# Latent attention: vector work of later head pairs on Pool, and an earlier split of the second output weight

## The reference, cut to what matters

```python
def mla(h, cos, sin, w_down, q_norm, w_uq, kv_norm, w_ukv, w_o):
    d = h @ w_down                                        # 384 + 128 + 64 columns
    cq = rms_norm(d[..., :Q_LORA_RANK], q_norm)
    ckv = rms_norm(d[..., Q_LORA_RANK:Q_LORA_RANK + KV_LORA_RANK], kv_norm)
    k_rope = apply_rope(d[..., Q_LORA_RANK + KV_LORA_RANK:], cos, sin)
    q = (cq @ w_uq).reshape(B, S, N_HEADS, QK_HEAD_DIM)   # per head 128 plain, 64 rotary
    q_rope = apply_rope(q[..., QK_NOPE_DIM:], cos[:, :, None], sin[:, :, None])
    kv = (ckv @ w_ukv).reshape(B, S, N_HEADS, QK_NOPE_DIM + V_HEAD_DIM)
    o = causal_attention(q, k, v)                         # 8 heads, 512 tokens
    return o.reshape(B, S, N_HEADS * V_HEAD_DIM) @ w_o    # 1024 x 1024
```

## Time and profile before

| | |
|---|---|
| median of the runs | 1404.18 us |
| the profiled execution's own time | 1406.12 us |
| its span in the trace | 1404.3 us |
| PE matmul busy | 1328.1 us, 95% |
| VectorE (DVE) busy | 788.8 us, 56% |
| ScalarE (ACT) busy | 536.7 us, 38% |
| Pool busy | 33.0 us, 2% |
| granted TensorE clock, mean | 0.983 |
| attention loop, first scores to last scores | about 445 to 553 us |
| output tiles, to the first tile of the third unit | to 589.4 us |

### The profile page before, as it was taken

One profiled execution on the slowest core, in us unless ns is written; L12 is line 12 of the kernel. 1 busy time (PEld: TensorE's weight loads), 2 busy tenths in 40 slices (PEclk: granted clock), 3 DMA queues, 4 the chain that ended last, 5 costly groups with the idle time before them and its releaser, 6 DMA issues.

```text
span 1404.3 us, 16380 instructions
## 1 busy us (share of the span) xinstructions
PE 1328.1 (95%) x6217; PEld 1099.4 (78%) x6217; DVE 788.8 (56%) x1098; ACT 536.7 (38%) x758; POOL 33.0 (2%) x32
## 2 busy tenths in 40 slices
PE   6999999999999888899999999999999999977997
PEld 5788888888877777788888888888887787766876
DVE  5644445444458676564444444545675578876554
ACT  6522233233334444332322222343233445555334
POOL 6000000000000000000000000000000000020000
PEclk9999999999999899999999999999999999979998
DMA  5122322222331100132222322325441211102321
GB/s 207 62 90 91 118 90 90 84 91 83 101 99 55 49 31 31 60 119 92 90 90 91 118 75 83 101 83 144 130 150 61 60 48 28 61 0 99 116 71 60
DMA packets 120888, 119.43 MB, mean 85 GB/s; under 512 B 13500, under 2 KB 117896, under 8 KB 120584
## 3 DMA queue, kind: packets, MB, share of 16 engines
q1 hardware_dynamic: 120840, 118.77, 26.3%
HBM read 114.57 MB, written 4.19 MB: 85 GB/s over the span
## 4 chain that ended last, share of the span: by engine, by line
PE 83%; DVE 9%; ACT 4%; issue 3%; SPq 0%; DMA 0%; DVEq 0%; ACTq 0%
PE psum L1649 25%; PE psum L1650 25%; PE psum L1651 25%; DVE w_lo L1049 1%; PE psum L1998 1%; ACT w_hi L614 1%; PE psum L1984 1%; PE psum L1970 1%; DVE xg_lo L1225 1%; PE psum L2056 1%; PE psum L1693 1%; DVE du L1326 0%; PE psum L2092 0%; DVE row_top L1250 0%; PE psum L1917 0%
## 5 line engine op out<-in xcount | busy, mean ns | idle before, releaser
L1649 PE MATMUL psum<-xg_hi,w_hi 128*128 128x512 f32 x1072 | 426.1, 397 | 2.1 <-DVE xg_lo L1563 2.1
L1651 PE MATMUL psum<-xg_hi,w_lo 128*128 128x512 f32 x1072 | 417.6, 390 | 0.0
L1650 PE MATMUL psum<-xg_lo,w_hi 128*128 128x512 f32 x1072 | 417.4, 389 | 0.0
L1649 PEld LDWEIGHTS psum<-xg_hi,w_hi 128*128 128x128 f32 x1072 | 201.6, 188 | 44.6 <-DVE xg_lo L1563 3.5
L1651 PEld LDWEIGHTS psum<-xg_hi,w_lo 128*128 128x128 f32 x1072 | 201.2, 188 | 42.5
L1650 PEld LDWEIGHTS psum<-xg_lo,w_hi 128*128 128x128 f32 x1072 | 201.5, 188 | 40.6 <-issue 1.4
L1112 DVE TENSOR_TENSOR w_lo<-w_raw,w_hi 128x2048 fp32r<-128x2048 f32 x42 | 96.3, 2292 | 154.4 <-ACT w_hi L667 154.4
L1136 DVE TENSOR_TENSOR w_lo<-w_raw,w_hi 128x2048 fp32r<-128x2048 f32 x32 | 73.3, 2292 | 115.9 <-ACT w_hi L686 115.9
L1649 PE MATMUL psum<-act_hi,w_hi 128*128 128x512 f32 x352 | 137.2, 390 | 0.0
L1651 PE MATMUL psum<-act_hi,w_lo 128*128 128x512 f32 x352 | 137.0, 389 | 0.0
L1650 PE MATMUL psum<-act_lo,w_hi 128*128 128x512 f32 x352 | 136.9, 389 | 0.0
(11 more groups left out here) (366 smaller groups left out, 1751.6 us busy)
## 6 DMA issues: line engine op xcount, KB each, us to landing
w_raw<-in_ffn_w_gate SPq DMA_DIRECT2D x22, 1024.0 KB, 5.0
w_raw<-in_ffn_w_up SPq DMA_DIRECT2D x22, 1024.0 KB, 5.0
w_raw<-in_w_in SPq DMA_DIRECT2D x16, 1024.0 KB, 5.5
w_raw<-in_ffn_w_down SPq DMA_DIRECT2D x16, 768.0 KB, 4.8
w_raw<-in_ffn_w_down SPq DMA_DIRECT2D x16, 640.0 KB, 4.5
w_raw<-in_mla_w_o SPq DMA_DIRECT2D x4, 1024.0 KB, 5.0
w_raw<-in_w_out SPq DMA_DIRECT2D x4, 1024.0 KB, 5.1
w_raw<-in_w_ple_gate SPq DMA_DIRECT2D x4, 1024.0 KB, 5.0
```

The source lines that it names most:

```text
L1649: pe.matmul(o, wh, xh, start=start, stop=False, skip_group_check=True)
L1650: pe.matmul(o, wh, xl, start=False, stop=False, skip_group_check=True)
L1651: return pe.matmul(o, wl, xh, start=False, stop=stop, skip_group_check=True)
```

## The change

For pairs 1 to 3, ScalarE copies the `u` projection out of PSUM into the SBUF tile `rope_in`, and Pool makes the four rotary products from it, one after the other with a wait between, and later the rotary residue of each head. Pool also makes the whole residue of the weight units of pairs 1 to 3 and of the first output unit, where VectorE made it in three pieces. VectorE keeps all of this for pair 0. The waits on PSUM banks follow: the bank of a `u` is free when the copy is made. The second output unit is split when the loop has issued the last scores (ScalarE at step 32, VectorE at step 33), and TensorE runs seven of the eight heads of `out(2)` before it finishes `out(0)` and `out(1)`.

```diff
+            def heads_split(n):
+                pool.wait_ge(lo_sem, n)
+                pool.wait_ge(hi_sem, n + 1)
+                c = slice(0, head_thirds(n)[-1])
+                pool.tensor_tensor(w_lo[:, n % 2, c], raw(n)[:, c], w_hi[:, n % 2, c].bitcast(F32), ALU.subtract).then_inc(lo_sem, 1)
+                pool.wait_ge(lo_sem, n + 1)
+            def rotary_products(pr):
+                pool.wait_ge(sem("rope_kept"), pr)
+                pool.wait_ge(sem("rope_lo"), 2 * pr)
+                for e in range(2):
+                    r = slice(64 * e, 64 * e + 64)
+                    for half, table in enumerate((cos_t, sin_t)):
+                        if e or half:
+                            pool.wait_ge(sem("rope_turned"), 4 * pr + 2 * e + half)
+                        pool.tensor_tensor(squares[64 * half:64 * half + 64, e, :], rope_in[r, :], table[r, :], ALU.mult)\
+                            .then_inc(sem("rope_turned"), 1)
+                pool.wait_ge(sem("rope_turned"), 4 * pr + 4)
+            def rotary_residue(h):
+                pool.wait_ge(sem("rope_hi"), h + 1)
+                pool.tensor_tensor(xg_lo[:, QR + h % 2, :], squares[:, h % 2, :], xg_hi[:, QR + h % 2, :].bitcast(F32), ALU.subtract)\
+                    .then_inc(sem("rope_lo"), 1)
+                pool.wait_ge(sem("rope_lo"), h + 1)
+            for h in range(HEADS):
+                for ii in range(NB):
+                    if rotary_head(h, ii) is not None:
+                        rotary_residue(rotary_head(h, ii))
+                    if (h // 2 + 1, "u") in after_step(h, ii):
+                        rotary_products(h // 2 + 1)
+                    if h % 2 == 0 and ii == 0:
+                        heads_split(FIRST["heads"] + 1 + h // 2)
...
                     if what == "u":
+                        if pr:
+                            act.wait_ge(sem("proj_done"), idx + 1)
+                            act.activation(rope_in, proj_result(idx), ACT.Copy).then_inc(sem("rope_kept"), 1)
                         return
...
-                    if h % 2 == 0:
-                        act.wait_ge(sem("rope_turned"), 3 * (h // 2) + 2)
-                    else:
-                        act.wait_ge(sem("proj_ready"), proj_count(h // 2, "u"))
+                    act.wait_ge(sem("rope_turned"), 2 * h + 2)
...
+                    if s == NB * HEADS:
+                        split_hi(FIRST["mla_o"] + 1)
...
-                        if rotary_head(h, ii) is not None:
-                            rotary(rotary_head(h, ii))
                         for t in after_step(h, ii):
                             proj(*t)
-                        if h % 2 == 0 and ii >= 1:
-                            split_lo(FIRST["heads"] + 1 + h // 2, ii - 1)
+                    if s == NB * HEADS + 1:
+                        dve.wait_ge(lo_sem, FIRST["mla_o"] + 1)
+                        split_lo(FIRST["mla_o"] + 1)
...
-                        pe.wait_ge(sem("proj_ready"), idx - 1 if idx > len(FIRST_PROJ) else 4)
+                        pe.wait_ge(*proj_released(idx - 2 if idx > len(FIRST_PROJ) else FIRST_PROJ.index("vb")))
...
+                out(2, 0, 7)
                 for m in range(KD):
-                    out(m, 6 if m < 2 else 0, HEADS)
+                    out(m, 6 if m < 2 else 7 if m == 2 else 0, HEADS)
```

More of the change, by code:

```diff
@@ L224, in program @@
         cos_s, sin_s = probs[:, 0, :], probs[:, 1, :]
+        rope_in = sq_sum2[:, :]
         QN, KN, VV, QR = 0, 2, 4, 6
@@ L332, in proj_count, with proj_index, proj_released @@
         def proj_count(pr, *whats):
-            return max(PROJ_ORDER.index((pr, what)) for what in whats) + 1
+            return max(proj_index(pr, what) for what in whats) + 1
+        def proj_index(pr, what):
+            return [x for x in PROJ_ORDER if x[1] != "u"].index((pr, what))
+        def proj_released(idx):
+            pr, what = PROJ_ORDER[idx]
+            if what == "u":
+                return (sem("rope_turned"), 4) if pr == 0 else (sem("rope_kept"), pr)
+            return sem("proj_ready"), proj_index(pr, what) + 1
         def proj_tiles(idx, x):
@@ L798, in mla @@
                 for u in range(1, 5):
-                    split_hi(FIRST["mla_o"] + u)
+                    if u > 1:
+                        split_hi(FIRST["mla_o"] + u)
                     for m in (2 * u - 2, 2 * u - 1):
@@ L1206, in proj @@
                     idx = PROJ_ORDER.index((pr, what))
-                    done = sem("proj_ready")
-                    if idx:
-                        dve.wait_ge(done, idx)
                     if what == "u":
[L1211 to L1214, removed]
+                        if pr == 0:
+                            dve.wait_ge(sem("proj_done"), idx + 1)
                             dve.wait_ge(sem("cq_sum"), 2)
[L1216 to L1221, removed]
+                            ps = proj_result(idx)
+                            for e in range(2):
+                                r = slice(64 * e, 64 * e + 64)
+                                for half, table in enumerate((cos_t, sin_t)):
+                                    dve.tensor_tensor(squares[64 * half:64 * half + 64, e, :], ps[r, :], table[r, :], ALU.mult)\
+                                       .then_inc(sem("rope_turned"), 1)
                         return
-                    hi = [x for x in PROJ_ORDER if x[1] != "u"].index((pr, what)) + 1
-                    dve.wait_ge(sem("proj_hi"), hi)
-                    dve.tensor_tensor(proj_tiles(idx, xg_lo), proj_result(idx), proj_tiles(idx, xg_hi).bitcast(F32), ALU.subtract).then_inc(done, 1)
+                    dve.wait_ge(sem("proj_hi"), proj_index(pr, what) + 1)
+                    dve.tensor_tensor(proj_tiles(idx, xg_lo), proj_result(idx), proj_tiles(idx, xg_hi).bitcast(F32), ALU.subtract)\
+                       .then_inc(sem("proj_ready"), 1)
                 def rotary(h):
@@ L1293, in mla @@
                 for u in range(1, 5):
-                    split_lo(FIRST["mla_o"] + u)
+                    if u > 1:
+                        split_lo(FIRST["mla_o"] + u)
                     for m in (2 * u - 2, 2 * u - 1):
@@ L1860, in out @@
                         if m < 2:
-                            pe.wait_ge(sem("proj_ready"), len(PROJ_ORDER))
+                            pe.wait_ge(sem("proj_ready"), len(PROJ_ORDER) - HEADS // 2)
                         elif m < 4:
```

## The result

| | median us | runs |
|---|---|---|
| before | 1403.58 | 6 (1400.3 to 1404.34) |
| after | 1412.38 | 6 (1407.62 to 1414.59) |

The ratio is 1.006 (95% interval 1.0047 to 1.0073): the change makes the kernel 8.8 us slower, outside the predicted range, though not by 2%. The profiled execution took 1412.35 us.

What follows compares the result with a forecast made beforehand. It took the stage to be bound by a chain through VectorE's order, TensorE being 95% busy. Terms +0.4 + 1.4 - 1.0 + 0.4 - 2.1 + 2.4 = +1.5 us gave 1405.7 us against the median, range 1400.5 to 1411.

Steps and rivals of the forecast that it cites:

- Pool's prices: Pool's subtractions and products: 1.28 us for 64x512 and 128x512, 4.0 for 1664 columns, 4.9 for 2048.
- Rival (b): Pool's serial rotary instructions slow down beside VectorE: about +11 us, 1415 us; chance 0.35 together with (c) and more clock falls.
- the 0.3 us a chain: Allowance in each Pool chain for Pool being held by about two VectorE normalisations, taken between none and 0.8 us.
- (a): VectorE's relief steadies the clock in the attention loop: -4.3 us, 1399.9 us; chance 0.21 including a weaker form.
- (c): Early output unit does nothing, costing 2.1 us: 1407.8 us; called unlikely, chance 0.35 together with (b) and more clock falls.
- Part 4: Output tiles: two waits totalling 3.7 us go, a new 1.6 us wait comes before out(4); net -2.1 us.
- Part 1: First weight unit's residue: Pool ends at 454.86 where VectorE released kn0 at 454.45; +0.4 us.
- Part 2: Rotary chain from behind u to even heads' scores: 8.03 us each, three times, costing +1.1, +0.3 and 0.0; +1.4 us.
- Part 3: Even halves, Pool's weight unit before the odd head's rotary residue: -0.5 in second and third pairs, +0.4 in the fourth.
- Part 5: Granted clock falls at two of the three 3.1 us gaps before even heads, 1.2 us each: +2.4 us.
- the marks that I set for being wrong: PE's waits before even heads under 2 us, VectorE's waits still leading, or Pool's products averaging over 1.5 us.

Runs made afterwards that it cites:

- experiment 1: Kernel before with only the early split of the second output unit and seven heads of out(2) moved ahead; 1404.59 us, ratio 1.0004.
- experiment 3: Changed kernel with weight residues back on VectorE in thirds, rotary products and residues still on Pool; 1400.91 us, ratio 0.9987.
- experiment 2: Kernel before with the early output split and weight residues on Pool, rotary work staying on VectorE; 1411.62 us, ratio 1.0061.
- experiment 6: Changed kernel with the row maximum's product taking its second factor as a per-partition scalar; 1403.76 us, ratio 1.001.
- experiment 10: Changed kernel with one-tile maximum and third output unit rounded sooner: weights on VectorE 1401.01 us; last kernel, weights on Pool, 1400.83 us.

## Why the prediction was wrong

**Pool's prices** were right or a little high. 64x512: 1.28 priced, 1.28 measured; 1664 columns 4.0, 3.87; 2048 columns 4.9, 4.58. Rival (b), Pool slower in company, did not happen: the products stayed at 1.26 to 1.29 us, and so the 0.3 us a chain that I took for a held Pool did not show. The Trainium skill's 4.5 us for 2048 columns (GPSIMD Engine Reference, section 3.1) was nearer than my 4.9. Of the others, (a) went the other way, the clock fell more often, and (c) did not come about, as Part 4 shows.

**Part 1** (+0.4). Pool's residue ended at 450.67 + 3.72 = 454.39, 0.5 before the forecast; but the normalisation that came up at 451.40 was held for 3.20 us, and the transpose that waited for it started at 454.66. From the second head's scores to the matmul behind `u` it is 8.48 us (451.32 to 459.80), 1.0 more than before (451.23 to 458.69).

**Part 2** (+1.4) was right in kind. From behind `u` to the even head's scores took 8.07, 7.73 and 7.72 us for a priced 8.03 each, so +1.1, 0.0 and -0.35 against the earlier trace rows. The three waits, each of which ends 0.1 us behind Pool's residue (467.77, 500.54, 534.48) and so is one for Pool, though the profile marks it issue:

```profile
467.87 0.47 PE L1697 MATMUL psum<-xg_hi 128*128 128x512 f32 x1 [2.79 <-issue]
...
500.64 0.77 PE L1697 MATMUL psum<-xg_hi 128*128 128x512 f32 x1 [1.46 <-issue]
...
534.58 0.76 PE L1697 MATMUL psum<-xg_hi 128*128 128x512 f32 x1 [1.46 <-issue]
```

Only the first is near the 3 us that I named. In front of the other two TensorE also waits 1.05 us for turned residues, behind a normalisation that was held for 1.45 us, so the gap is in two pieces. (The 4.9 us of matmuls in that sum are 5.0 by its own terms.) By experiments 1 and 3 the whole rotary move was worth -1.1 in the rest, not +1.4: its relief of VectorE was counted at nothing, and may be what pays for the longer chain.

**Part 3** (-0.6 for three halves) is **the step that failed**, and in it the sentence "VectorE, relieved, has the `qn1` residue at about 511.7, so Pool is last here too". VectorE started it at 515.97, because the product and the normalisation in front of it were held. I had read in the earlier trace rows that Pool was held by VectorE's subtraction, priced 0.3 for that direction, and never asked for the other: what VectorE would have to run while Pool was inside a 4 us instruction. I left the holding of VectorE out of every term of the sum. The weight move, which Parts 1 and 3 put at -0.2, was worth +3.7 in the rest with the rotary part on Pool (experiment 3 against after) and +6.5 without (experiment 2 against 1). The larger part of the same step's loss stands in Part 5.

The Trainium skill says it outright (SBUF — State Buffer, Who interferes with whom): the port pair of the two engines is an exclusive lock, which the one that starts first keeps for its whole instruction, and a VectorE instruction with two SBUF inputs contends with a Pool instruction that reads SBUF. The trace agrees: 1.07 us where 0.16 is usual, ending with Pool's. The Trainium skill says there too that VectorE instructions with at most one SBUF input outside the two-port modes do not contend; here the one-tile product took 0.21 us in the midst of Pool's 4.00. I had used the shorter statement of the rule and let it act on Pool alone.

**Part 4** (-2.1) was right: 19.46 to 17.35 us, with the two waits gone and the new one where it was placed, 1.5 us for a priced 1.6:

```profile
595.39 0.50 PE L1697 MATMUL psum<-o_hi,w_hi 128*128 128x512 f32 x1 [1.54 <-DVE w_lo L1102]
```

Why the rest fell by 3.3 in experiment 1, 1.2 more than this, is open.

**Part 5** (+2.4) missed its main cause: the shortfall grew by 8.6. With the product freed (experiment 6) it is 23.0, +2.2 against before, so 6.4 come with the holding of that product. The 2.2 that are left look like the 2.4 that I charged for the gaps before the even heads, but these runs do not show that they are: the tail alone, without such gaps, has 24.3, and the last kernel of experiment 10, with all of them, 21.0. Two of the falls stand at these waits: TensorE's wait of 1.91 us at 516.19 above, and this one in the fourth pair, where the held product took 1.74 us:

```profile
551.17 1.09 PE L1888 MATMUL psum<-ident,probs 128*128 128x128 f32 x4 [2.76 <-DVE pt_lo L1315]
```

The clock was 0.50 from 516.7 to 520.1 and from 550.8 to 554.2 us. In this execution the two of Pool's gaps that I charged 1.2 us each cost at most 0.46 x 7 = 3.2 and 0.47 x 7 = 3.3:

```profile
500.00:507.00 7.00, 6.36 (x22) 5.53 (x23) 2.99 (x9) 2.29 (x6) 0.54 (x1) 0.54 0.01 2
534.00:541.00 7.00, 6.42 (x22) 5.58 (x23) 2.94 (x9) 2.28 (x6) 0.48 (x1) 0.53 0.01 2
```

In both stretches before ran at 1.00, behind waits of 1.01 us. But in experiment 6 the second of these gaps is longer (2.79 us at 499.16) and the same seven microseconds had 0.76, and behind the third, 2.79 us at 529.51, there was no fall. Why one wait is followed by a fall and another is not, these runs do not show; that the one edit of experiment 6 takes 6.4 us of shortfall away, they do.

**The sum.** Parts 1 to 4 together were -0.9, and the rest moved by -0.7; but that agreement is luck, two errors against each other: the weights moved the rest by 3.9 more than I had said, rotary part and tail by 3.7 less. The clock term was 2.4 for 8.6. Of the marks that I set for being wrong two came: VectorE's waits still lead the list, and two of the three waits before even heads are under 2 us (1.46), though not because Pool was faster than priced.

## What to carry to other kernels

Before work goes to Pool, list what VectorE runs during each Pool instruction, and look there for two SBUF inputs or an SBUF-to-SBUF operation: size does not protect it, since a 128x1 product waits for the end of a 4 us instruction (1.07 us here, 1.74 with one of 4.6). What matters is what waits behind the held instruction: here the exponential behind the row maximum, in experiment 2 the residues of turned probabilities, which come behind the rotary residue in VectorE's order. Give such a small instruction one tensor operand (8.6 us here), or cut Pool's long ones in pieces (5.6); and compare the mean length of untouched instructions before and after, since the chain of waits and the list of releasers name VectorE, not Pool. On a TensorE-bound kernel split each run into the clock's shortfall and the rest: here the change did nearly nothing to the second and lost 8.6 us in the first.

## What the runs showed of the hardware that was not expected

- A 128x1 product of two SBUF operands was held for up to 1.6 us (1.74 for 0.16), a subtraction of 128x512 for 3.1 (3.80 for 0.69, experiment 2), a normalisation of 128x384 for 2.8 (3.20 for 0.42), each ending with Pool's instruction or up to 0.55 us behind it. The same product with a per-partition scalar took 0.21 us beside Pool.
- Being held once leads to being held again: Pool's next instruction starts 0.08 us after the last, ahead of what VectorE has next (514.23 before 514.28). Seven of the eight held normalisations of the changed kernel follow a held product.
- The mean clock moved the time more than the waits did: 0.985 before and 0.979 after, 8.6 us, with 3.7 us more of waits in the loop.
